# The beginning of a two-block kernel: thin columns in one tile, the first unit block by block, sums of squares later, one split on GpSimd

## The reference

```python
h = rmsnorm(x, norm_mix_g[l])            # x * rsqrt(mean(x*x) + EPS) * g
proj = h @ w_in[l]                       # 1024 -> bg, cg, xv, q, k, v, z, a, b, ga, gb
...
qkv = jax.nn.silu(causal_dwconv(jnp.concatenate([q, k, v], axis=-1), conv_w))
...
beta = jax.nn.sigmoid(b.astype(f32))
g = -jnp.exp(A_log.astype(f32)) * jax.nn.softplus(a.astype(f32) + dt_bias.astype(f32))
...
G = jnp.cumsum(g, axis=-1)
decay = jnp.exp(jnp.where(tril, G[..., :, None] - G[..., None, :], -jnp.inf))
```

## Time and profile before

| what | us |
|---|---|
| median of 3 runs (1270.0 to 1270.39) | 1270.17 |
| the profiled execution: its span, first to last instruction | 1268.4 |
| TensorE busy | 1253.7 (99%) |
| VectorE busy | 832.6 (66%) |
| ScalarE busy | 578.6 (46%) |
| GpSimd busy | 223.9 (18%) |

### The profile page before, as it was taken

One profiled execution on the slowest core, in us unless ns is written; L12 is line 12 of the kernel. 1 busy time (PEld: TensorE's weight loads), 2 busy tenths in 40 slices (PEclk: granted clock), 3 DMA queues, 4 the chain that ended last, 5 costly groups with the idle time before them and its releaser, 6 DMA issues.

```text
span 1268.4 us, 20147 instructions
## 1 busy us (share of the span) xinstructions
PE 1253.7 (99%) x6633; PEld 1007.2 (79%) x6633; DVE 832.6 (66%) x1705; ACT 578.6 (46%) x1049; POOL 223.9 (18%) x476
## 2 busy tenths in 40 slices
PE   8999999999999999999999999999999999999998
PEld 6787878878788788888888888888888767777776
DVE  6978777787676843444477773367765686794743
ACT  5664545545455432223344442244444455666632
POOL 2603314032140400001300000000004124440021
PEclk9999999999999999999999999999999999999999
DMA  6345263453534433333233323433224334333221
GB/s 182 84 117 136 75 155 88 120 124 83 141 94 120 125 92 108 99 99 100 83 100 99 99 73 90 118 100 99 81 79 113 102 108 126 83 84 100 80 70 67
DMA packets 283492, 130.01 MB, mean 103 GB/s; under 512 B 77296, under 2 KB 276271, under 8 KB 283445
## 3 DMA queue, kind: packets, MB, share of 16 engines
q1 hardware_dynamic: 283445, 129.42, 37.3%
HBM read 119.34 MB, written 10.06 MB: 102 GB/s over the span
## 4 chain that ended last, share of the span: by engine, by line
PE 95%; DVE 2%; issue 1%; ACT 1%; DMA 0%; SPq 0%; POOLq 0%; DVEq 0%; POOL 0%; ACTq 0%
PE gb L833 82%; PE gb L1279 2%; PE gd L1279 1%; PE gd L1229 1%; PE gd L1219 1%; PE gd L1207 1%; PE gd L925 1%; PE gd L933 1%; PE gd L1005 1%; PE gd L1016 1%; PE gd L994 0%; PE gd L993 0%; PE gd L1012 0%; PE gb L1207 0%; PE gd L1186 0%
## 5 line engine op out<-in xcount | busy, mean ns | idle before, releaser
L833 PE MATMUL gb<-act_a,whi 128*128 128x512 f32 x2656 | 888.8, 398 | 0.3 <-DVE wlo L1818 0.2
L833 PEld LDWEIGHTS gb<-act_a,whi 128*128 128x128 f32 x2656 | 498.9, 188 | 112.0 <-issue 9.9
L833 PE MATMUL gb<-act_a,wlo 128*128 128x512 f32 x1408 | 548.9, 390 | 0.0
L1818 DVE TENSOR_TENSOR wlo<-raw,whi 128x1024 fp32r<-128x1024 f32 (+1 forms) x197 | 235.8, 1197 | 134.6 <-ACT whi L1329 132.5
L1329 ACT ACTIVATE whi<-raw 128x1024 fp32r<-128x1024 f32 (+1 forms) x210 | 216.1, 1029 | 216.9 <-PE gb L833 191.7
L833 PEld LDWEIGHTS gb<-act_a,wlo 128*128 128x128 f32 x1408 | 265.1, 188 | 48.2 <-issue 0.5
L833 PE MATMUL gb<-act_b,whi 128*128 128x512 f32 x432 | 152.5, 393 | 0.0
L833 PEld LDWEIGHTS gb<-act_b,whi 128*128 128x128 f32 x432 | 81.1, 188 | 17.3 <-DVE qc L2112 0.4
L2711 POOL TENSOR_TENSOR zs<-zs,ca 128x512 f32<-128x512 f32 x3 | 4.2, 1395 | 321.3 <-ACT ca L1332 321.3
L833 PE MATMUL gb<-act_b,wlo 128*128 128x512 f32 x128 | 49.9, 390 | 0.0
L2666 POOL TENSOR_TENSOR Ue<-Ue,elt 128x60 f32<-128x60 f32 (+14 forms) x120 | 45.0, 375 | 9.4
(11 more groups left out here) (487 smaller groups left out, 1497.3 us busy)
## 6 DMA issues: line engine op xcount, KB each, us to landing
raw<-in_w_in_dram SPq DMA_DIRECT2D x102, 512.0 KB, 3.7
raw<-in_w_up_dram SPq DMA_DIRECT2D x44, 512.0 KB, 3.6
raw<-in_w_down_dram SPq DMA_DIRECT2D x16, 384.0 KB, 3.1
raw<-in_w_down_dram SPq DMA_DIRECT2D x16, 320.0 KB, 3.0
raw<-in_w_a_out_dram SPq DMA_DIRECT2D x8, 512.0 KB, 4.2
raw<-in_w_b_out_dram SPq DMA_DIRECT2D x8, 512.0 KB, 3.5
raw<-in_w_o_dram SPq DMA_DIRECT2D x8, 512.0 KB, 3.4
raw<-in_w_out_dram SPq DMA_DIRECT2D x8, 512.0 KB, 3.5
```

The source lines that it names most:

```text
L833: ins = pe.matmul(gb[:, b, :], l, r, start=(first and m == 0), stop=(last and m == len(todo) - 1))
L1818: dve.tensor_tensor(wlo[:, i % 2, 0:k * P], raw[:, i % 4, 0:k * P], whi[:, i % 2, 0:k * P].bitcast(F32), ALU.subtract).then_inc(split_read ...
```

## The change

- **Thin columns in one tile.** The low part of the 16 thin weights is put into columns 16 to 31 of each block of `whi`, behind the high part. One product then gives high and low weights at once (32 output rows), so a block needs two products (with the high and with the low half of x) and not three. ScalarE copies 32 rows. The turn back becomes a product with `ide`, a 0/1 matrix with two ones in each column, which adds row c and row c+16.
- **First unit block by block.** Unit N_B is cut in eight parts with a wait for each block's low half. Four parts come before the thin products of blocks 4 to 7, one behind them, two behind the parameters' transposes, one behind the turn of a and b. The spread of the norm moves into unit N_B+1.
- **Its split earlier.** ScalarE's and VectorE's split of N_B stand behind block 3 and no longer behind block 7; ScalarE's copies to `xT` of blocks 4 to 7 come behind all the high halves.
- **Sums of squares later.** Two of VectorE's stay between the blocks, four come behind block 7; ScalarE has two, ahead of its copy of the thin result. VectorE's copy of the parameters comes behind its split of N_B+1.
- **GpSimd splits the third unit** (N_B+2, `POOL_EARLY`), which VectorE skips; the scalings of x wait for `ab_g`. ScalarE splits that unit before it keeps `first_row`.

```diff
-        def thin(t):
-            return t.rearrange("p (k n) -> p k n", k=KD)[:, :, 0:AB_COLS]
+        def thin(t, at=0, n=AB_COLS):
+            return t.rearrange("p (k n) -> p k n", k=KD)[:, :, at:at + n]
...
         POOL_SPLITS = range(N_Z + 9, N_Z + 22)
+        POOL_EARLY = N_B + 2
         plan = schedule()
...
                 pe.wait_ge(raw_lo, k + 1)
-                hi = whi[:, N_AB, k * P:k * P + AB_COLS]
-                lo = wlo[:, N_AB, k * P:k * P + AB_COLS]
-                a, c = slot(YB_HI + k), slot(YB_LO + k)
-                pe.matmul(gb[0:AB_COLS, 3, :], hi, a, start=(k == 0), stop=False)
-                pe.matmul(gb[0:AB_COLS, 3, :], lo, a, start=False, stop=False)
-                ins = pe.matmul(gb[0:AB_COLS, 3, :], hi, c, start=False, stop=(k == KD - 1))
+                both = whi[:, N_AB, k * P:k * P + 2 * AB_COLS]
+                pe.matmul(gb[0:2 * AB_COLS, 3, :], both, slot(YB_HI + k), start=(k == 0), stop=False)
+                ins = pe.matmul(gb[0:2 * AB_COLS, 3, :], both, slot(YB_LO + k), start=False, stop=(k == KD - 1))
                 if k == KD - 1:
...
             turn_x(7)
-            for k in range(3, KD):
+            thin_products(3)
+            first = unit(N_B, N_B, 0, 0, YB_HI, YB_LO, parts=KD, ready=(raw_lo, 0))
+            for k in range(4):
+                next(first)
+            for k in range(4, KD):
                 thin_products(k)
+            next(first)
             pe.wait_ge(par_landed, 16 * PAR_DMAS)
...
             ins.then_inc(par_turned, 1)
-            for m, _ in enumerate(unit(N_B, N_B, 0, 0, YB_HI, YB_LO, parts=4)):
-                if m == 0:
-                    pe.wait_ge(ab_ready, 1)
-                    for c in range(TC):
-                        ins = pe.transpose(gd[:, 0, c * P:c * P + AB_COLS], ob[0:AB_COLS, c, :],
-                                           ident[0:AB_COLS, 0:AB_COLS])
-                    ins.then_inc(ab_turned, 1)
-                elif m == 2:
-                    pe.wait_ge(par_ready, 2)
-                    norm_spread(0)
+            next(first)
+            next(first)
+            pe.wait_ge(ab_ready, 1)
+            for c in range(TC):
+                ins = pe.matmul(gd[:, 0, c * P:c * P + AB_COLS], ob[0:2 * AB_COLS, c, :], ide[0:2 * AB_COLS, :],
+                                start=True, stop=True)
+            ins.then_inc(ab_turned, 1)
+            for _ in first:
+                pass
...
                         next(u)
+                        if peeled and (s, m) == (1, 0):
+                            pe.wait_ge(par_ready, 2)
+                            norm_spread(0)
                         if peeled and s == 1 and m == 3:
...
-            for k in range(KD):
+            def x_copy(k):
                 sc.wait_ge(x_turned, k + 1)
                 sc.activation(xT[:, k, :], x_bank(k), ACT.Copy).then_inc(xT_ready, 1)
+            def x_high(k):
+                sc.wait_ge(x_turned, k + 1)
+                sc.activation(slot(YB_HI + k), x_bank(k), ACT.Copy, scale=par[:, R_MIX_G + k:R_MIX_G + k + 1]).then_inc(raw_hi, 1)
+            for k in range(4):
+                x_copy(k)
                 if k == 0:
                     sc.wait_ge(par_ready, 1)
-                sc.activation(slot(YB_HI + k), x_bank(k), ACT.Copy, scale=par[:, R_MIX_G + k:R_MIX_G + k + 1]).then_inc(raw_hi, 1)
+                x_high(k)
                 if k == 1:
...
             split(N_B, N_B)
+            for k in range(4, KD):
+                x_high(k)
+            for k in range(4, KD):
+                sc.wait_ge(raw_lo, k + 1)
+                x_copy(k)
...
-            token_squares(1)
-            sc.wait_ge(unit_done, 1)
-            sc.activation(flat(ob)[0:AB_COLS, :], gb[0:AB_COLS, 3, :], ACT.Copy).then_inc(ab_ready, 1)
             token_squares(2)
             token_squares(3)
+            sc.wait_ge(unit_done, 1)
+            sc.activation(flat(ob)[0:2 * AB_COLS, :], gb[0:2 * AB_COLS, 3, :], ACT.Copy).then_inc(ab_ready, 1)
             split(N_B + 1, N_B + 1)
...
             sc.activation(sm[:, 4, 0:HEADS], rows8[:, 0:HEADS], ACT.Exp).then_inc(ab_exp, 1)
+            split(N_B + 2, N_B + 2)
             sc.wait_ge(norm_turned, SPREAD_AT[0])
             sc.activation(first_row, gd[:, 1, :], ACT.Copy).then_inc(row_kept, 1)
-            split(N_B + 2, N_B + 2)
...
-                if isinstance(n, int) and n in POOL_SPLITS:
+                if isinstance(n, int) and (n in POOL_SPLITS or n == POOL_EARLY):
                     return
                 dve.wait_ge(hi_ready, n + 1)
-                if isinstance(n, int) and n - 1 in POOL_SPLITS:
+                if isinstance(n, int) and (n - 1 in POOL_SPLITS or n - 1 == POOL_EARLY):
                     dve.wait_ge(split_ready, n)
...
             dve.wait_ge(par_ready, 1)
+            def late_squares(c):
+                junk = (kc[:], flat(AT))[c]
+                dve.tensor_tensor_reduce(junk, xin[:, c, T:2 * T], xin[:, c, T:2 * T], 1.0, 0.0, ALU.mult, ALU.add,
+                                         ss[:, 1, c:c + 1]).then_inc(x_squared, 1)
             for k in range(KD):
+                if k == 4:
+                    split(N_B, N_B)
                 raw_low(k)
...
                     dve.wait_ge(hi_ready, 1)
-                    dve.tensor_tensor(thin(wlo[:, N_AB, :]), thin(raw[:, N_AB, :]), thin(whi[:, N_AB, :]).bitcast(F32),
+                    dve.tensor_tensor(thin(whi[:, N_AB, :], AB_COLS), thin(raw[:, N_AB, :]), thin(whi[:, N_AB, :]).bitcast(F32),
                                       ALU.subtract).then_inc(split_ready, 1)
...
                     dve.wait_ge(x_landed[1], 16)
-                if 1 <= k <= 4:
+                if 1 <= k <= 2:
                     token_squares(k - 1)
-                elif k == 5:
-                    dve.wait_ge(x_landed[2], 16)
-                    dve.wait_ge(x_landed[3], 16)
-                    dve.tensor_tensor_reduce(kc[:], xin[:, 0, T:2 * T], xin[:, 0, T:2 * T], 1.0, 0.0, ALU.mult, ALU.add,
-                                             ss[:, 1, 0:1]).then_inc(x_squared, 1)
-            split(N_B, N_B)
+            dve.wait_ge(x_landed[2], 16)
+            dve.wait_ge(x_landed[3], 16)
+            token_squares(2)
+            token_squares(3)
+            for c in range(2):
+                late_squares(c)
             dve.wait_ge(x_squared, TC)
...
             mean_square().then_inc(xss_ready, 1)
+            split(N_B + 1, N_B + 1)
             dve.wait_ge(par_turned, 2)
...
             dve.wait_ge(par_ready, 2)
-            split(N_B + 1, N_B + 1)
...
             pool.wait_ge(xT_ready, KD)
-            pool.wait_ge(split_ready, N_B + 3)
+            pool.wait_ge(split_ready, POOL_EARLY)
+            pool.wait_ge(hi_ready, POOL_EARLY + 1)
+            pool.tensor_tensor(wlo[:, POOL_EARLY % 2, :], raw[:, POOL_EARLY % 4, :],
+                               whi[:, POOL_EARLY % 2, :].bitcast(F32), ALU.subtract).then_inc(split_ready, 1)
+            pool.wait_ge(ab_g, 1)
             def scale_x(k):
```

## The result

The changed kernel takes 1272.99 us (median of 14 runs, 1272.68 to 1273.47), the kernel before 1270.20: a ratio of 1.0022, 95% interval 1.0015 to 1.0029. It is 2.8 us slower. The prediction of 1271.4 us had the sign and the kind of mechanism, but the loss is more than double the 1.2 us that it forecast, and 1272.99 lies above the stated range. The profiled execution has

The account below looks back on a forecast made before the run. VectorE's queue was taken to bound the kernel from the a/b chain on: 1.4 us late less 0.2 idle gives 1.2, so span 1269.6 us plus 1.8 is 1271.4 us; range 1268.1 to 1272.4 us.

Parts of the forecast that it names:

- VectorE's queue leads, TensorE's gain is handed back: Up to 76 us: VectorE's queue decides what comes out; TensorE's 2.1 us gain at the ab_g wait is lost again.
- 0.36 us of waiting at Rr: At 75.93 us in the earlier trace: TensorE idle until VectorE's Rr was there, read as VectorE leading.
- The chain is held by GpSimd's split: a/b chain: GpSimd's split, 24.3 to 26.7 us, holds a VectorE instruction; ab_g at about 29.6 us, 2.0 later.
- The small tap copies: Behind ab_g: held up to 1.05 us by the first scaling if at all, adding nothing on VectorE.
- The hold of the split of N_B+3: Behind the taps: the split waits for the fourth scaling from 33.8 until 34.9 us and ends 1.78 us late.
- The chain's start: VectorE's a/b chain starts at 21.13 us against 21.40 before, 0.27 us earlier.
- The turn of a and b: On TensorE: four full f32 products, taken as 0.6 us, bounds 0.34 to 0.9, with no effect.
- The load of N_B: Unit N_B's weights land by 10.35 us at the latest, needed by 10.58: in time by 0.23 us.
- the wait for `ab_g`: TensorE ends unit N_B+1 at about 27.6 us against 29.74 and arrives here 2.1 us earlier.
- The idle 0.20 us at 58.02: VectorE's wait for TensorE at 58.02 us goes, taking 0.2 us off its 1.4 us lateness.
- the first rival: a/b chain: 32-column instructions are not held; VectorE comes out 1.9 us early, 1268.3 us; chance 0.17.

Follow-up runs that it names:

- x5: Changed kernel with GpSimd's split undone and the turn of a and b ahead of two parts of unit N_B; 1270.00 us.
- x6: Changed kernel, GpSimd's split undone, only two N_B parts ahead of thin blocks 4 to 7, turn and parameters' copy earlier; 1268.89 us.
- x9: x6 with unit N_B's weights loaded ahead of the last quarter of x; 1268.46 us.
- x3: Changed kernel with the five tap copies of head 0 moved from behind ab_g to ahead of the a/b chain; 1271.74 us.
- x11: Changed kernel with GpSimd's split undone and a GpSimd memset of 2560 columns where it stood; 1273.58 us.
- x10: Changed kernel with GpSimd's split of N_B+2 in four instructions of 256 columns; 1272.88 us.
- x4: Changed kernel with the turn of a and b ahead of the two parts of unit N_B before it; 1272.58 us.
- x2: Kernel before with only GpSimd's split of N_B+2, scalings waiting for ab_g, ScalarE's split of it ahead of first_row; 1272.67 us.

## Why the prediction was right in kind and wrong in size

- **VectorE's queue leads, TensorE's gain is handed back.** Right. x5, x6 and x9 moved the time by about what they moved the chain's start or the taps (0.7 for 0.88, 1.3 for 1.15 and 1.29, 1.7 for 1.47 us). It holds while the clock is full: in the profiled runs of x3 and x11 TensorE led. The row that I took as the proof, 0.36 us of waiting at Rr, proves less than I said: the wait is 0.35 to 0.37 us in every run, in these two as well.
- **The chain is held by GpSimd's split.** Right: 3.63 - 1.55 = 2.08 us measured; I had a delay of 2.88 + 26.7 - 27.3 = 2.3. GpSimd's split started at 25.48 us, outside the 24.0 to 24.8 that I had given, but it hangs on ScalarE's exponentials and so on the chain's start, and moved with it, so it met the chain at the same place. The instruction held was a SCALAR_TENSOR_TENSOR in the changed kernel and a TENSOR_SCALAR in x3; it made no difference, as said. The Trainium skill (SBUF — State Buffer, Who interferes with whom) has both kinds, and that whichever came first keeps the other out for a whole instruction: the trace agrees (3.63 against 1.55 us, 2.40 against 0.18), and x10 shows that cutting the instruction doesn't help.
- **The small tap copies: the step that failed.** I put them at 0 to 1.05 us, by the first scaling alone, and argued that the next hold would swallow it, so that they counted nothing in the sum. Two copies were held, by the first and by the second scaling: 33.04 - 30.22 = 2.82 us from the chain's last step to the rescaling, where 0.70 were counted, so 2.1 us. The four scalings follow each other without a gap, so an instruction that waits is let in only between two, and the next one meets the next scaling. I counted collisions for each GpSimd instruction on its own and not for each of VectorE's in the queue. The hold of the split of N_B+3 that I had in the sum (1.1 us) did not occur, because VectorE came after the scalings were over; without it the forecast would have been farther off. x3 moved the copies and took 2.6 us off VectorE's queue, 2.1 by the holds and 0.5 by their own time.
- **The chain's start.** Forecast 21.13, measured 22.15. The turn of a and b was bounded at 0.34 to 0.9 us "with no effect": it takes 0.99 us and ends last (0.59 us of idle time before the chain; x4, x5). The load of N_B was "in time, by 0.23 us"; ScalarE waited 0.24 us for it. Besides, the whole profiled run starts 0.15 us later, and TensorE's 20 products up to the thin result took 4.73 us and not 4.56.
- **TensorE.** It came to the wait for `ab_g` at 28.9 us, not 27.6, for the same two reasons; this cost nothing, because `ab_g` came at 30.4.
- **The idle 0.20 us at 58.02** The earlier trace rows did not go, since TensorE was late by the same amount there.
- In all: 0.8 us by the chain's start and its hold and 2.1 by the copies, less 1.1 for the hold that did not come, and 0.2 for the idle time that stayed make 2.0 more at 79 us than the 1.2 of the forecast, 3.2 measured; 0.3 came back at the end.
- **A slip in the first rival.** Its own terms add up to 1.5 + 0.37 + 0.20 = 2.1 us early, not 1.9; nothing hangs on it, since the instructions were held.

## What to carry to other kernels

Work moved to GpSimd is not free where VectorE has, beside it, instructions that read two SBUF tensors or take one from SBUF to SBUF (COPY, TENSOR_SCALAR): 1.14 us taken off VectorE cost 2.5 us here (x2). Before such a move, walk VectorE's queue instruction by instruction through GpSimd's busy stretch; a row of back-to-back GpSimd instructions takes its toll from each short VectorE instruction that it meets, and cutting a long one into pieces changed little (x10). Where two engines are full, the one that the other waits for at the end of the stretch (here at Rr) is the one whose queue must get shorter or start earlier. And look at the granted clock behind each stretch in which TensorE idles: in the profiled runs of x3 and x11 TensorE idled for VectorE, and the half clock that followed cost it another 1.6 us, which made it the leading engine. The page's 40 slices don't show it; a table of short stretches does.

## What the runs showed of the hardware

- A memset on GpSimd, which reads nothing, held a TENSOR_SCALAR of 32 columns on VectorE for the memset's length (2.27 us against 0.18). A RECIPROCAL of the chain was not beside a GpSimd instruction in any run here.
- TensorE's granted clock fell to half in two profiled runs: from 32.0 to 35.4 us in x3, 1.4 us of work after an idle time of 1.77 us, and from 32.3 to 35.6 us in x11, right behind idle times of 1.60 and 1.08 us with 0.6 us of work between them. It stayed full in the changed kernel after an idle time of 1.58 us.
- A VectorE instruction that waits is let in after the running GpSimd instruction, and GpSimd goes on right behind it: with four pieces the seven still lost 1.8 us.
- A product of plain f32 with 16 columns takes 0.25 us of TensorE (0.99 for the four), where the turn by transposes took 0.34 for four.
- The profile can name the wrong releaser of a wait for several semaphores: 0.59 us were put down to VectorE's own copy and ended with TensorE's turn.
